# A decoder step with state-space, sparse attention and sixteen experts: a second fixed expert, another order of loads, compressed probabilities turned four heads at once, an output projection that starts at half rows

## The reference

```python
o_c = einsum(p_c, v_c); o_s = ...; o_w = ...          # compressed, selected, window attention, 8 heads of 64
o_nsa = g0 * o_c + g1 * o_s + g2 * o_w
merged = sigmoid(g_a) * (glu @ w_ssm_out) + sigmoid(g_b) * (o_nsa @ w_nsa_out)
x = x + merged @ w_o
h = rms_norm(x)                                       # experts: top 1 of 4 groups, top 2 of 4 experts in it
act = silu(h @ w_gate[e]) * (h @ w_up[e]) * weight[e]  # 16 experts, 1024 -> 256
x = x + sum over the 2 chosen of act @ w_down[e]      # 256 -> 1024
x = x + sigmoid(x @ w_ple_gate) * (p @ w_ple)
y = rms_norm(x)
```

## Time and profile before

| | |
|---|---|
| median of 3 runs | 825.48 us (824.95 to 826.32) |
| the profiled execution, whole | 828.95 us |
| its span on the core | 827.2 us |
| TensorE busy | 792.4 us, 96% |
| VectorE, ScalarE, GpSimd busy | 344.8, 195.2, 138.9 us |
| DMA | 136.50 MB |

### The profile page before, as it was taken

The page is one execution under the profiler, slowest core; times in us unless marked ns, Lnnn a source line. Parts: engine busy times, 40 slices in busy tenths (PEclk is TensorE's granted clock), DMA queues, the critical chain, the costliest instruction groups (busy, mean ns, idle before and its releaser), DMA issues. The chain is left out here.

```text
span 827.2 us, 13746 instructions
## 1 busy us (share of the span) xinstructions
PE 792.4 (96%) x5169; PEld 511.4 (62%) x5169; DVE 344.8 (42%) x940; ACT 195.2 (24%) x462; POOL 138.9 (17%) x164
## 2 busy tenths in 40 slices
PE   8999999999999999989999999999899999899995
PEld 5455678877778888545566774445566555444441
DVE  3289901455553323666634372114631110115333
ACT  3010201310012354655433100045111111112222
POOL 3039200500003011334500100011200110014000
PEclk9999999999999999998999999999999999999998
DMA  9530393453302597500030474013799999897011
GB/s 331 134 122 0 116 277 142 132 43 97 128 29 69 124 211 210 156 1 1 1 116 2 119 264 159 1 50 116 311 415 417 416 419 415 331 377 233 26 51 39
DMA packets 81222, 136.50 MB, mean 165 GB/s; under 512 B 33926, under 2 KB 57546, under 8 KB 76946
## 3 DMA queue, kind: packets, MB, share of 16 engines
q1 hardware_dynamic: 64636, 110.17, 40.3%
q0 software_dynamic: 3728, 13.38, 4.5%
q10 hardware_dynamic: 12798, 12.12, 4.4%
HBM read 116.55 MB, written 21.19 MB: 167 GB/s over the span
## 5 line engine op out<-in xcount | busy, mean ns | idle before, releaser
L1165 PE MATMUL ps<-hT,w_slot 128*128 128x288 f32 x640 | 156.2, 407 | 0.0
L1165 PEld LDWEIGHTS ps<-hT,w_slot 128*128 128x128 f32 x640 | 121.3, 190 | 34.1 <-issue 0.8
L1165 PE MATMUL ps<-w_slot,hT 128*128 128x512 f32 (+1 forms) x320 | 127.1, 555 | 0.6 <-DVE hT L1827 0.3
L1165 PEld LDWEIGHTS ps<-w_slot,hT 128*128 128x128 f32 x320 | 60.0, 190 | 61.5 <-issue 42.4
L1165 PE MATMUL ps<-w_slot,merged 128*128 128x512 f32 x128 | 56.0, 594 | 1.1 <-DVE merged L2142 1.1
L2613 DVE SCALAR_TENSOR_TENSOR th<-th,ps 128x256 f32<-128x256 f32 x12 | 5.1, 421 | 108.6 <-ACT th L2069 108.6
L1669 PE MATMUL ps<-w_slot,hT 128*32 128x256 f32 x544 | 49.9, 379 | 0.0
L1165 PEld LDWEIGHTS ps<-w_slot,merged 128*128 128x128 f32 x128 | 23.9, 190 | 29.9 <-issue 28.2
L1165 PE MATMUL ps<-qg,w_slot 128*128 128x288 f32 x128 | 33.7, 408 | 0.0
L1039 POOL TENSOR_TENSOR hT<-hT,w_p 128x512 f32<-128x512 f32 (+3 forms) x11 | 25.1, 2282 | 50.4 <-DVE w_p L2142 50.4
L2399 DVE TENSOR_REDUCE nm_p<-ps 128x2 f32<-128x256 f32 (+3 forms) x32 | 25.0, 819 | 17.6 <-PE ps L1408 17.6
(11 more groups left out here) (440 smaller groups left out, 1217.3 us busy)
## 6 DMA issues: line engine op xcount, KB each, us to landing
merged<-in_w_exp_down SPq DMA_DIRECT2D x11, 1024.0 KB, 17.2
w_slot<-in_w_in SPq DMA_DIRECT2D x8, 1024.0 KB, 7.0
wgu<-in_w_exp_gate SPq DMA_DIRECT2D x8, 1024.0 KB, 15.2
wgu<-in_w_exp_up SPq DMA_DIRECT2D x8, 1024.0 KB, 18.4
w_slot<-in_w_exp_gate SPq DMA_DIRECT2D x8, 1024.0 KB, 13.7
w_slot<-in_w_exp_up SPq DMA_DIRECT2D x8, 1024.0 KB, 16.3
expert_rows<-onsaT ACTq DMA_DIRECT2D x12, 512.0 KB, 8.6
w_slot<-in_w_exp_down SPq DMA_DIRECT2D x5, 1024.0 KB, 20.6
```

What stands on the lines that cost most here:

```text
L1165: ins = pe.matmul(out, a, b, start=(n == 0), stop=(n == len(pairs) - 1))
```

## The change

- `first_at` pins experts 0 and 1 to columns 0 and 1. Gate, up and down of both are asked for with fixed numbers, before the order of the experts is known; before, only those of expert 0.
- Column 1 holds 96 rows, and its pass takes column 12 as a second; the other columns move (`RANK_OF_COLUMN`, `COLUMNS_OF_PASS`, `LOADED`, the tables), and the order of loads in the loop with them. Column 3 now has a pass of its own.
- `pg0` is asked for ahead of the last down load and inside the loop, `pg1` only after the two gathers of tile 0 have landed.
- Compressed probabilities: one transpose of 128 x 128 (four heads of 32) instead of four of 128 x 32; `vcp` becomes 128 x 2 x 128 with each head's 32 rows on partitions of their own and zeros elsewhere, so that the value product is two of 128 rows and 128 columns in place of two of 32 rows, 64 wide, 256 columns. `vcp` is made by four products into the four quarters of the partitions, a memset and four copies.
- `through_w_o` of tiles 0 and 1 waits for 15 merged halves, the others for 16.
- In pass 0 the turn of pass 1's rows comes after the fourth k step of the up product, not ahead of its first.

```diff
-RANK_OF_COLUMN = [0, 1, 5, 6, 2, 7, 8, 3, 9, 10, 14, 4, 11, 12, 13, 15]
-COLUMNS_OF_PASS = [[0], [1], [2, 12], [3, 12], [4], [5, 13], [6, 13], [7], [8, 14], [9, 14], [10, 15], [11]]
+RANK_OF_COLUMN = [0, 1, 6, 2, 7, 8, 3, 9, 10, 4, 14, 5, 11, 12, 13, 15]
+COLUMNS_OF_PASS = [[0], [1, 12], [2, 12], [3], [4, 13], [5, 13], [6], [7, 14], [8, 14], [9], [10, 15], [11]]
 NPASS = len(COLUMNS_OF_PASS)
 OF_PARITY = [-(-NPASS // 2), NPASS // 2]
-LOADED = [0, 1, 2, 12, 3, 4, 5, 13, 6, 7, 8, 14, 9, 10, 15, 11]
+LOADED = [0, 1, 12, 2, 3, 4, 13, 5, 6, 7, 14, 8, 9, 10, 15, 11]
...
-                vcp = sb("vcp", [32, P], stack=at)
+                vcp = sb("vcp", [P, 2, P], stack=at)
...
-            load_gate_up(0, 0)
+            for u in range(2):
+                load_gate_up(u, u)
...
-            load_down(0, 0)
+            for u in range(2):
+                load_down(u, u)
             sp.wait_ge(order_made, 1)
-            at_column = {0: 0}
+            at_column = {0: 0, 1: 1}
...
-            for l in range(1, NX):
+            for l in range(2, NX):
                 read_column(l)
                 load_gate_up(l, expert(l))
-            load_down(1, expert(1))
...
                 down_weights(3)
                 gate_up_weights(6)
+                gate_up_weights(7)
                 down_weights(4)
-                gate_up_weights(7)
                 gate_up_weights(8)
                 down_weights(5)
+                down_weights(6)
                 gate_up_weights(9)
-                down_weights(6)
                 down_weights(7)
                 gate_up_weights(10)
+                gate_up_weights(11)
                 down_weights(8)
-                gate_up_weights(11)
                 gate_up_weights(12)
                 down_weights(9)
+                down_weights(10)
                 gate_up_weights(13)
-                down_weights(10)
                 down_weights(11)
                 gate_up_weights(14)
+                gate_up_weights(15)
                 down_weights(12)
-                gate_up_weights(15)
                 down_weights(13)
                 down_weights(14)
-                down_weights(15)
                 sp.wait_ge(g_done, j * NPASS + (NPASS - 1))
                 sp.sem_inc(slot_free, 1)
+                load_weights("pg0")
+                down_weights(15)
+                for c in range(2):
+                    sp.wait_ge(yg_ld[0][c], j * 48 + 16)
+                sp.sem_inc(slot_free, 1)
                 with sp.If(j + 1 < rounds):
 
+                    sp.wait_ge(w_need["pg0"][0], j * 16 + w_need["pg0"][1])
+                    sp.sem_inc(slot_free, 1)
                     sp.wait_ge(x2_made, j * NT + 2 * NT)
                     sp.sem_inc(slot_free, 1)
                     for l in range(3):
                         load_gate_up(l, expert(l))
                         load_down(l, expert(l))
                     load_gate_up(3, expert(3))
-            load_weights("pg0")
...
-            row_of(base_at[:, 12:15], 2 * CAP + 96, 3 * CAP)
+            row_of(base_at[:, 12:15], CAP + 96, 3 * CAP)
...
+            for at, cap in ((slice(0, 1), 128), (slice(1, 3), 96), (slice(3, 4), 128), (slice(4, 6), 96), (slice(6, 7), 128),
+                            (slice(7, 9), 96), (slice(9, 10), 128), (slice(10, 11), 64), (slice(11, 12), 128), (slice(12, 16), 64)):
...
-            pool.memset(first_at[:, 0:1], float(2 ** 21))
-            row_of(first_at[:, 1:NE], NE - 2, -1)
-            for at in (slice(0, 2), slice(2, 4), slice(4, 5), slice(5, 7), slice(7, 8), slice(8, 10), slice(10, 11), slice(11, 12),
-                       slice(12, 15), slice(15, 16)):
+            for e in range(2):
+                pool.memset(first_at[:, e:e + 1], float(2 ** (21 - e)))
+            row_of(first_at[:, 2:NE], NE - 3, -1)
...
-                    pe.matmul(ps[0:32, 7, 0:P], cx[:, 1, 1, CJ_P:CJ_P + 32], w2[:, 1], start=True, stop=True).then_inc(cmp_made, 1)
+                    for g in range(4):
+                        ins = pe.matmul(ps[32 * g:32 * g + 32, 7, 0:P], cx[:, 1, 1, CJ_P:CJ_P + 32], w2[:, 1], start=True, stop=True)
+                    ins.then_inc(cmp_made, 1)
...
-                    for kh in range(NKV):
+                    if c == "c":
+                        ins = pe.transpose(ps[:, 4 + at % 2, 0:P], pc[:, P * half:P * half + P], ident[:])
+                    for kh in range(NKV if c != "c" else 0):
                         for k in range(2):
                             to = P * (2 * kh + k)
-                            if c == "c":
-                                src = 32 * (2 * (2 * half + k) + kh)
-                                ins = pe.transpose(ps[0:32, 4 + at % 2, to:to + P], pc[:, src:src + 32], ident[:])
-                            else:
-                                src = (2 * k + kh) * n + P * c
-                                ins = pe.transpose(ps[:, 4 + at % 2, to:to + P], probs[i % PBUFS][:, src:src + P], ident[:])
+                            src = (2 * k + kh) * n + P * c
+                            ins = pe.transpose(ps[:, 4 + at % 2, to:to + P], probs[i % PBUFS][:, src:src + P], ident[:])
                     ins.then_inc(pr_turned, 1)
                 elif what == "v":
                     at = VALUE_OF[i, c]
@@ -1448,13 +1455,13 @@
                     if (i, c) == (2, "c"):
                         pe.wait_ge(cmp_taken, COMPRESSED["vcp", 0])
                     vcol = KVW * r + P
-                    rows = 32 if c == "c" else P
-                    for kh in range(NKV):
+                    for k in range(2 if c == "c" else 0):
+                        to = 256 * half + P * k
+                        ins = pe.matmul(ps[:, 6 + b % 2, to:to + P], vcp[:, k], ptp[:, at % PTS, 0:P], start=False, stop=True, skip_group_check=True)
+                    for kh in range(NKV if c != "c" else 0):
                         lo = HD * kh
-                        v = vcp[0:32, lo:lo + HD] if c == "c" else kv[:, c, vcol + lo:vcol + lo + HD]
-                        ins = pe.matmul(ps[lo:lo + HD, 6 + b % 2, 256 * half:256 * half + 256], v,
-                                        ptp[0:rows, at % PTS, 256 * kh:256 * kh + 256], start=first, stop=(r == 1 and c == "c"),
-                                        skip_group_check=True)
+                        ins = pe.matmul(ps[lo:lo + HD, 6 + b % 2, 256 * half:256 * half + 256], kv[:, c, vcol + lo:vcol + lo + HD],
+                                        ptp[:, at % PTS, 256 * kh:256 * kh + 256], start=first, stop=False, skip_group_check=True)
...
-            pe.wait_ge(merged_made, 2 * KD)
             def through_w_o(t, c):
                 p = TILES[t]
                 o = begin(("wo", t, c))
                 pe.wait_ge(*w_need[f"wo{c}"])
+                pe.wait_ge(merged_made, 2 * KD - (1 if P * t + p <= HALF else 0))
...
-                    if w and between:
-                        between()
                     for k in range(KD):
+                        if w and k == 4 and between:
+                            between()
...
-                    pe.wait_ge(*w_need[f"pg{c}"])
+                    if c:
+                        pe.wait_ge(*w_need["pg1"])
+                    else:
+                        pe.wait_ge(w_need["pg0"][0], rounds * 16 + (w_need["pg0"][1] - 16))
...
-            rows = 32 if c == "c" else P
+            cols = P if c == "c" else 4 * P
             n = VALUE_OF[i, c]
             if n >= PTS:
                 eng.wait_ge(pr_values, n - PTS + 1)
-            copy(ptp[0:rows, n % PTS], ps[0:rows, 4 + at % 2, :]).then_inc(pr_took[TAKEN_BY[i, c][0]], 1)
+            copy(ptp[:, n % PTS, 0:cols], ps[:, 4 + at % 2, 0:cols]).then_inc(pr_took[TAKEN_BY[i, c][0]], 1)
...
+                    link(dve.memset(vcp[:], 0.0))
                     for h in range(NKV):
                         dve.tensor_copy(kcbd[HD * h:HD * h + HD, h], ps[HD * h:HD * h + HD, 6, CJ_P:CJ_P + 32])
                     ins = dve.tensor_copy(kc[:], ps[:, 6, 0:NBLK])
                 elif what == "vcp":
-                    ins = dve.tensor_copy(vcp[:], ps[0:32, 7, 0:P])
+                    for g in range(4):
+                        at, lo = slice(32 * g, 32 * g + 32), HD * (g % 2)
+                        ins = dve.tensor_copy(vcp[at, g // 2, lo:lo + HD], ps[at, 7, lo:lo + HD])
```

More of the change, by code:

```diff
@@ L1060, in _ @@
                 pool.memset(split_at[:, at], float(split))
-            pool.memset(first_at[:, 0:1], float(2 ** 21))
-            row_of(first_at[:, 1:NE], NE - 2, -1)
-            for at in (slice(0, 2), slice(2, 4), slice(4, 5), slice(5, 7), slice(7, 8), slice(8, 10), slice(10, 11), slice(11, 12),
-                       slice(12, 15), slice(15, 16)):
+            for e in range(2):
+                pool.memset(first_at[:, e:e + 1], float(2 ** (21 - e)))
+            row_of(first_at[:, 2:NE], NE - 3, -1)
+            for at in (slice(0, 2), slice(2, 3), slice(3, 4), slice(4, 6), slice(6, 7), slice(7, 9), slice(9, 10), slice(10, 11),
```

(3 more changed lines are left out.)

2 lines of the change are left out of this document (removed).

## The result

The changed kernel takes 820.13 us (median of 10 runs, 817.33 to 823.97), the kernel before 825.89 in the same group of runs (10 runs): a ratio of 0.9926, 95% interval 0.9905 to 0.9947. That is 5.8 us faster, about half of the 11.7 forecast and outside its range of 810 to 819.

What follows compares the result with a forecast made beforehand. TensorE, busy 792.4 of 827.2 us, was taken as the bound, with DMA as a second limit in the expert passes; 3.0 + 1.1 + 1.1 + 4.3 + 2.2 = 11.7 us off gave 813.8, range 810 to 819.

Steps and rivals of the forecast that it cites:

- holds the second half until the gathers of tile 0 have landed ... Gain 2.2: At the end, keeping w_ple_gate's second half off tile 0's gather removes TensorE's wait for x: 2.2 us gained.
- The rival on w_ple_gate: At the end, the held second half lands after TensorE wants it: 3.0 us lost, 816.8; chance 0.03, of which 0.02 slower.
- Compressed probabilities: In the prompt attention, fewer transposes, reshaped value products and smaller copies: sum 3.2 us, taken as 3.0.
- so I price this at nothing: At vcp, four copies make VectorE some 0.5 us later, covered by the turn's saving: no cost; 0.5 without cover.
- What had been said of unit 14: In the prompt attention, unit 14's turn stands just ahead of a 0.46 us wait for GpSimd: no gain counted.
- the hidden memset of vcp: On VectorE at "kc", the memset is covered by TensorE's eight further products: no cost; 0.5 us without cover.
- The rival "the clock": In the prompt attention, half speed once more, 816.7, chance 0.10; or the stretch vanishes, 810.9, chance 0.07.
- Weights: In the expert passes, landings 5.1 to 7.6 us earlier cut later weight waits: 4.3 of 5.0 us gained.
- the rival "loads as late as before": In the expert passes, landings follow slots coming free, not bytes ahead: 4.3 us stay away, 818.1; chance 0.12.
- Waits below 1 us in sum: Sign in the profile after: TensorE's waits for weights in the expert passes sum to below 1 us.
- Half rows: At w_o, tiles 0 and 1 start on the finished merged half, removing the whole wait on merged: 1.1 us.
- rows of pass 1: In pass 0, turning these rows four k steps later lets them land in time: 1.1 us gained.

Runs made afterwards that it cites:

- a_pg1: Changed kernel with w_ple_gate's second half issued as soon as its buffer is free, not held back: 818.69 us, ratio 0.9908 to the kernel before.
- b_att: Kernel before with only the compressed probabilities' part (vcp and pc) added: 824.85 us against 826.29, ratio 0.9973.
- a_vcp1: Changed kernel with vcp made by one VectorE product with a 0/1 mask instead of memset and four copies: 819.00 us, ratio 0.9920 to the kernel before.
- b_rows: Kernel before with only the two moved waits (w_o on half rows, later turn of pass 1's rows): 824.37 us against 826.29, ratio 0.9981.
- a_pg1_again: Repeat of the changed kernel without holding back w_ple_gate's second half: 818.66 us, ratio 0.9917 to the kernel before.
- a_vcs: Changed kernel with the products for vcs moved behind the turns of unit 2: 819.48 us, ratio 0.9926 to the kernel before.
- a_best2: Changed kernel with w_ple_gate's second half not held, the mask product for vcp and two load-order places set back: 818.75 us, ratio 0.9922 to before.
- a_best3: Changed kernel with a_best2's three edits and vcs's products behind the turns of unit 2: 816.86 us, ratio 0.9906 to the kernel before.
- a_late2: Changed kernel with the second fixed expert's weights asked for only once the order is known: 825.40 us, ratio 0.9990 to the kernel before.
- b_end1: Kernel before with w_ple_gate's first half loaded ahead of down load 15, second half not held: 831.74 us against 826.15, ratio 1.0072.
- b_again: The kernel before, unchanged, for a second profile: 826.43 us (1 run), against 826.29.
- a_again: The changed kernel, unchanged, run again as base of its group: 820.52 us, ratio 0.9929 to the kernel before.
- a_again2: The changed kernel, unchanged, run again in the last group: 821.39 us, ratio 0.9943 to the kernel before.
- b_end: Kernel before with w_ple_gate's loads alone as in the change, second half held back: 831.79 us against 826.15, ratio 1.0076.
- b_load: Kernel before with the second fixed expert, new load order and w_ple_gate's new places, second half held: 823.64 us against 826.29, ratio 0.9965.

## Why the prediction was wrong

**The end, the largest miss.** The step that failed is "holds the second half until the gathers of tile 0 have landed ... Gain 2.2". Tile 0's wait did go. But the prediction followed x for tile 0 only and did not ask what the held load would meet: pass 11's rows, on which tile 1's gather hangs. A wait of 2.2 us became one of 1.8 to 2.8 elsewhere, so there was no gain. a_pg1 and its repetition show the cause: without the holding back tile 1's wait is gone. The rival on w_ple_gate named a late load, not this. How much the gather gains when the load stays away was open in the prediction: by bytes, 5.1 us. Issue to VectorE's start took 5.5 us in the mean of the eight profiles with the load held and 9.5 in the mean of the four without: holding back was worth 4.0 to it. By the rule of the Trainium skill (DMA: Bandwidth & Descriptors, "Queues, rings and completion order") I had reckoned 1.3, and 0.9 of tile 0's wait left; the measurement is nearer to the bytes, and no wait was left.

**Compressed probabilities, 3.0 forecast, 1.5 in the traces** (2.2 by b_att's time, 0.7 to 3.6). Two terms were mis-sized: a turn gives 0.31 and not 0.45 (the busy time of four short transposes was divided by four, though one alone takes 0.29, not 0.15), the products nothing and not 0.11 (a bound that the text had named). And the step "so I price this at nothing" failed: vcp's four copies take 0.91 instead of 0.27 us, TensorE waits 0.63 us longer, and a_vcp1 shows that the loss reaches the scores of the next block. What had been said of unit 14 held: its turn gave nothing, GpSimd's wait grew from 0.46 to 0.74. So did the hidden memset of vcp: TensorE reaches vcp's product as late after the first compression product as before.

**The clock.** The profiled time was taken down to the median by a fixed 3.47 us, but the half-speed stretch at 371 us was treated as the kernel's, and the rivals gave 0.07 to its going. It comes and goes: 1.2 instead of 2.4 GHz is granted near 370 us in ten of the 18 profiles (the first of before, b_rows, a_pg1, a_pg1_again, a_vcp1, a_vcs, a_best2, a_best3, a_late2, b_end1) and not in the other eight, b_again and the changed kernel's first among them. The prediction says that the trace has one such stretch; it has a second, right behind its wait of 2.2 us for x, and b_again has none there.

```profile
740.00:750.00 10.00, 7.78 (x20) 3.26 (x18) 3.04 (x4) 2.15 (x4) 4.35 (x7) 0.83 0.99 360
```

What the change does is lower the clock a little in the mean. Over the runs of the kernel before in the four groups and all those of the changed kernel, the mean granted clock of the span is 0.9945 before (82 runs) and 0.9932 after (26 runs); 0.996 or more was granted to 27 of the 82 and 1 of the 26. At half speed a busy stretch loses half of its length, so the loss is at most (1 - clock) x span: 4.6 and 5.6 us, some 1.0 more. Where it comes from is argued and not shown. The new stretch at 330 to 340 us stands right behind the longer wait for vcp in b_att, a_again and a_again2, but five other profiles with that same wait do not have it. For a link with long waits speaks that the three kernels with the longest ones have the lowest mean clocks: a_late2 0.9905, b_end 0.9898, b_end1 0.9907. The rival "the clock" had the right kind, at another place and a third of the size.

**Weights, 4.3 forecast.** The first profile says 1.1 us, and would have misled. Over the profiles with the old loads the waits sum to 5.0, 5.4, 5.6 and 6.3 (before, b_again, b_att, b_rows), over those with the change's loads, order and moved waits to 3.9, 2.0, 1.4, 1.7, 1.4, 0.8 and 0.6 (first profile, a_again, a_again2, a_vcp1, a_vcs, a_pg1, a_pg1_again): 5.6 against 1.7, a gain of 3.9. With the three profiles of the changed kernel itself alone it is 5.6 against 2.4, a gain of 3.2, and b_load, without the moved waits, has 3.1 us left. So the step held within this scatter, and the rival "loads as late as before" did not come true. "Waits below 1 us in sum" came true in two of the seven.

**Half rows 1.1, rows of pass 1 1.1.** Both waits went as forecast, 1.27 and about 1.1 us in the trace. By b_rows part or all of the second is given back where the loads are not earlier too.

**The sum** by what was measured: 1.5 + 1.3 + 1.1 + 3.9 - 0.9 (the end) - 1.0 (clock) = 5.9, against 5.8 with an interval of about 4.4 to 7.8. The end counts tile 1's wait, mean 2.4, against tile 0's, mean 1.6 over the four profiles with the old loads (2.2, 2.0, 1.0 and 1.0 in before, b_again, b_att and b_rows). So near an agreement is partly luck: with 3.2 for the weights the sum is 5.2, and the clock's 1.0 is a difference of two upper bounds. Why waits for weights differ so much from one execution to the next, from 1.4 to 3.9 us in three of the same program, stays open.

## What to carry to other kernels

When a load is held back to clear the way for one transfer, list what else it will then meet, up to the last transfer that someone waits for; in this kernel the load did least harm when issued before the critical writes and not between them. Profile a kernel two or three times before a wait or a slow stretch of a single execution goes into a sum. A part of a change that costs 6 us by itself can be harmless inside the whole, so try parts in both directions: added to the old kernel and taken from the new. And where a wait of some microseconds appears, look at the clock behind it: what it costs can be more than its length.

## What the runs showed of the hardware

A f32 transpose of 128x128 alone keeps TensorE busy 0.29 us, four of 128x32 in a row 0.60, so that merging four into one gave back half and not three quarters. A copy of 32x64 on VectorE takes 0.218 us and one of 32x128 0.27, so four of the smaller cost 0.91: here the number of copies counts far more than their width. Tile 0's second gather, 0.5 MB, took 5.3 to 5.9 us with w_ple_gate's second half held back and 8.8 to 10.2 with that load of 2 MB beside it.

Behind one and the same wait of 1.29 us TensorE fell to half speed in b_att, a_again and a_again2 but not in the changed kernel's first profile, which is the same program as the last two: so a stretch is not a fixed property of a program. Behind the waits of 3.75 and 4.05 us in b_end and b_end1 the first four records took 3.78 us in both, where 1.88 is usual. What stands ahead of a stretch seems to shift the odds, but no run isolates it.
